# A hybrid decoder layer on one core: projection quarters handed out in pieces during the sparse attention

## The reference

```
o_cmp: softmax over 63 compressed keys (computed ahead, outside the loop changed here)
o_slc: softmax over the selected blocks of 64 keys among all keys up to the row's own
o_win: softmax over a window of 512 keys
o = gt[0] * o_cmp + gt[1] * o_slc + gt[2] * o_win
```

## Time and profile before

| | us |
|---|---|
| median of three runs (lowest, highest) | 2026.82 (2026.44, 2088.94) |
| the profiled execution's own time | 2009.73 |
| its span, first to last instruction | 2007.6 |
| PE busy in the span | 1955.3 (97%) |
| DVE busy in the span | 1342.2 (67%) |
| ACT busy in the span | 928.1 (46%) |
| POOL busy in the span | 612.7 (31%) |

### The profile page before, as it was taken

One profiled execution on the slowest core, in us unless ns is written; L12 is line 12 of the kernel. 1 busy time (PEld: TensorE's weight loads), 2 busy tenths in 40 slices (PEclk: granted clock), 3 DMA queues, 4 the chain that ended last, 5 costly groups with the idle time before them and its releaser, 6 DMA issues. The chain is left out here.

```text
span 2007.6 us, 32329 instructions
## 1 busy us (share of the span) xinstructions
PE 1955.3 (97%) x9421; PEld 1474.9 (73%) x9422; DVE 1342.2 (67%) x2558; ACT 928.1 (46%) x1615; POOL 612.7 (31%) x403
## 2 busy tenths in 40 slices
PE   8999999999999999999999989999999999999996
PEld 7887787877768766658868647777777777677772
DVE  2794643444206677789867838788778787777776
ACT  2111221234212244451034347777777777677764
POOL 2443232223322221002142733333333333233321
PEclk9999999999999999999999999999999999999998
DMA  6122312132532211047770577999999999999986
GB/s 205 42 70 88 105 43 63 43 87 56 123 101 80 85 53 33 22 135 260 241 292 34 204 275 233 312 377 343 327 344 325 352 326 343 317 319 333 342 270 178
DMA packets 170899, 390.66 MB, mean 195 GB/s; under 512 B 27937, under 2 KB 100930, under 8 KB 146113
## 3 DMA queue, kind: packets, MB, share of 16 engines
q1 hardware_dynamic: 132032, 302.71, 41.6%
q0 software_dynamic: 29568, 70.09, 14.0%
q10 hardware_dynamic: 9216, 16.78, 2.2%
HBM read 338.58 MB, written 81.84 MB: 209 GB/s over the span
## 5 line engine op out<-in xcount | busy, mean ns | idle before, releaser
L649 PE MATMUL a_bank<-x_hi,w_hi 128*128 128x512 f32 x928 | 372.9, 402 | 0.0
L649 PE MATMUL a_bank<-x_hi,w_lo 128*128 128x512 f32 x928 | 362.4, 390 | 0.0
L649 PE MATMUL a_bank<-x_lo,w_hi 128*128 128x512 f32 x928 | 361.5, 390 | 0.0
L2368 DVE TENSOR_TENSOR u_lo<-w_gu,u_hi 128x1024 fp32r<-128x1024 f32 x225 | 268.1, 1219 | 37.6 <-ACT u_hi L2010 29.6
L2010 ACT ACTIVATE u_hi<-w_gu 128x1024 fp32r x225 | 230.6, 1065 | 19.2 <-SPq L1497 18.7
L584 POOL CAST w_hi<-w_raw 128x1024 fp32r<-128x1024 f32 x56 | 64.8, 1158 | 560.2 <-PE a_bank L649 539.5
L2383 DVE TENSOR_TENSOR d_lo<-w_d,d_hi 128x1024 fp32r<-128x1024 f32 x150 | 177.1, 1222 | 83.0 <-ACT d_hi L2118 81.0
L1800 PE MATMUL e_bank<-u_hi,x_g_hi 128*128 128x512 f32 x450 | 207.5, 461 | 0.0
L649 PEld LDWEIGHTS a_bank<-x_hi,w_hi 128*128 128x128 f32 x928 | 174.3, 188 | 40.7 <-issue 6.1
L649 PEld LDWEIGHTS a_bank<-x_hi,w_lo 128*128 128x128 f32 x928 | 174.2, 188 | 37.8
L649 PEld LDWEIGHTS a_bank<-x_lo,w_hi 128*128 128x128 f32 x928 | 174.6, 188 | 33.9 <-issue 0.5
(11 more groups left out here) (397 smaller groups left out, 3657.3 us busy)
## 6 DMA issues: line engine op xcount, KB each, us to landing
w_gu<-in_moe_wg SPq DMA_DIRECT2D x64, 1024.0 KB, 8.5
w_gu<-in_moe_wu SPq DMA_DIRECT2D x64, 1024.0 KB, 27.2
w_d<-in_moe_wd SPq DMA_DIRECT2D x64, 1024.0 KB, 25.5
w_raw<-in_w_in SPq DMA_DIRECT2D x53, 512.0 KB, 3.9
gates<-gate_out ACTq DMA_DIRECT2D x64, 256.0 KB, 2.0
g_sb<-gates SPq DMA_DIRECT2D x16, 1024.0 KB, 5.5
acc_odd<-zero POOLq DMA_DIRECT2D x9, 512.0 KB, 14.9
work<-in_w_out SPq DMA_DIRECT2D x4, 1024.0 KB, 8.1
```

The lines of the kernel that those rows point to most:

```text
L649: ins = pe.matmul(bank[h][:, :], w[:, c % 2, k, :], x[:, k, cols], start=(k == 0 and j == 0), stop=(k == KD - 1 and j == 2))
L2368: dve.tensor_tensor(up_part(u_lo[j]), up_weights(slot, j), up_part(u_hi[j]).bitcast(F32), ALU.subtract).then_inc(u_lo_dve, 1)
```

## The change

In the NSA loop the quarters go out in pieces of one contraction slice (three matmuls) each. The schedule gets items `('mm_k', q, k)` for the four pieces of quarter q, and the item `('mm', q)` behind the fourth, at which PE no longer computes anything but ACT and POOL do what they did. The number of pieces behind the groups of pair k-1 is 120 (four times the quarters left) times the pair's weight over 99. The weight of a pair is one plus its number of groups, and 99 is the sum over the first 30 pairs. The sliding-window loop keeps whole quarters at rate 2. Rounds -1 and 0 of NSA keep `adv(1)`.

```diff
-    state = dict(q=4, fill=0, pv=0)
+    state = dict(q=4, k=0, fill=0, pv=0)
...
+
+    def adv_k(n):
+        for _ in range(n):
+            if state['q'] < last:
+                items.append(('mm_k', state['q'], state['k']))
+                state['k'] += 1
+                if state['k'] == 4:
+                    items.append(('mm', state['q']))
+                    state['q'], state['k'] = state['q'] + 1, 0
...
-    def attention(pairs, rate):
+    def attention(pairs, rate, step):
...
-                    debt += rate / len(groups)
-                    adv(int(debt))
+                    debt += rate(pairs, k) / len(groups)
+                    step(int(debt))
                     debt -= int(debt)
...
-    attention(SWA, 2.0)
+    attention(SWA, lambda pairs, k: 2.0, adv)
...
-    attention(NSA, (last - state['q']) / (len(NSA) - 2))
-    adv(last)
+    pieces = 4 * (last - state['q'])
+    weight = [1 + (pr['nb'] + 1) // 2 for pr in NSA]
+    attention(NSA, lambda pairs, k: pieces * weight[k - 1] / sum(weight[:-2]), adv_k)
+    adv_k(4 * last)
     return items
 
 
 SCHEDULE = schedule()
+PIECES_FROM = next(item[1] for item in SCHEDULE if item[0] == 'mm_k')
...
-            def quarter(q):
+            def quarter(q, ks=range(4)):
 
                 c, h, part = q // 4, q // 2 % 2, q % 2
-                if q == 0:
-                    pe.wait_ge(w_first_hi, 1)
-                    pe.wait_ge(w_first_lo, 1)
-                elif q == 1 or q % 4 == 0:
-                    pe.wait_ge(w_hi_ready, c + 1)
-                    pe.wait_ge(w_lo_ready, c + 1)
-                if q < 4:
-                    pe.wait_ge(x_lo_ready, 4 * q + 4)
-                if part == 0 and c >= 1:
-                    pe.wait_ge(half_out, 2 * c + h - 1)
-                for k in range(4 * part, 4 * part + 4):
+                if 0 in ks:
+                    if q == 0:
+                        pe.wait_ge(w_first_hi, 1)
+                        pe.wait_ge(w_first_lo, 1)
+                    elif q == 1 or q % 4 == 0:
+                        pe.wait_ge(w_hi_ready, c + 1)
+                        pe.wait_ge(w_lo_ready, c + 1)
+                    if q < 4:
+                        pe.wait_ge(x_lo_ready, 4 * q + 4)
+                    if part == 0 and c >= 1:
+                        pe.wait_ge(half_out, 2 * c + h - 1)
+                for k in (4 * part + i for i in ks):
...
-                if part == 1:
+                if part == 1 and 3 in ks:
                     ins.then_inc(half_done, 1)
...
                 if what == 'mm':
-                    quarter(item[1])
+                    if item[1] < PIECES_FROM:
+                        quarter(item[1])
+                elif what == 'mm_k':
+                    quarter(item[1], item[2:])
```

## The result

The changed kernel takes 2027.81 us (median of 20 runs, 2023.80 to 2093.24) against 2025.07 us of the kernel before on the same chip (median of 20, 2019.23 to 2090.49). The ratio is 1.0019 with a 95% interval of 1.0012 to 1.0026: 3.8 us slower, where 5 us faster were forecast. In part of the executions of either kernel the clock is lower in the first 500 us and the time some 63 us longer; ratios leave these out, and the loop, which lies behind that stretch, can be read in them too.

A forecast was written before the change was run, and what follows sets the result against it. PE, busy 97% of the span, and its waits were taken as the bound. Gains of 10.0 us less 2.2, 1.6 and 0.8 made 5.4, called 5: from the median 2026.82 to 2021.8 us, range 2004 to 2031.

The forecast's parts named there:

- Prices on PE: PE times read from the trace: matmul spacing 0.232 us, a lone piece 0.87 including 0.17 for breaking off and resuming.
- step 1: Rounds 1 to 28: 34 groups without a quarter get pieces that fill PE's wait for ACT's copy; 7.9 us gained.
- Step 2: Three pieces leave rounds 1 to 28 for round 29: 2.1 us less on PE up to pair 30's scores.
- Step 3: Early rounds stripped of pieces become shorter on PE than on DVE in rounds 1, 4, 7, 8, 12: 2.2 us lost.
- Step 4: Round 29 with three pieces takes 6.8 us, DVE starts pair 31 later, and the loop's end is 1.6 us later.
- Step 5: POOL's splits hold DVE multiplies in rounds 1 to 8: 0.8 us more than before, 2.8 at most.
- PE's clock stayed at 1.00 ... so early waits of 0.5 us should not move it: PE's clock held at the 2.4 GHz level even where busy 7.74 of 10 us; no cost put on it.
- DVE held by POOL: Line 1217 in rounds without slack: seven splits may each hold a multiply 1.4 us; 4 us slower, 2031; chance 0.08.
- The gain is eaten: A cut costs 0.15 us more, 5.1 in all, or branch loads come 4 us late: 2026 to 2027; chance 0.22.
- a piece over 1.0 us: Sign of a wrong forecast: a lone piece takes over 1.0 us from its first matmul to the product.
- waits past round 16: Sign of a wrong forecast: a round past 16 shows PE waiting for DVE's line 1217.
- late loads: Sign of a wrong forecast: the first branch projections behind the loop wait for loads; up to 4 us given back.

The follow-up runs named there:

- the even kernel: Changed kernel with four pieces in every round instead of shares by weight: 2017.19 us, ratio 0.9965 to the kernel before.
- the kernel without holds: Changed kernel with POOL's subtraction cut to one of eight slices for every split in the loop, plus 12 dummy transposes ahead of pair 30: 2013.45 us (one run).
- the dummies: 12 transposes that nobody reads, added ahead of pair 30's first group; on the changed kernel 2024.07 us, ratio 1.000 to the kernel before.
- The shorter subtraction: Changed kernel, POOL's subtraction on one of eight slices for every split in the loop, with dummy transposes ahead of pair 30: 2013.45 us (one run).
- the short subtraction: Changed kernel with POOL's subtraction cut to one of eight slices, the loop's first split spared, no added dummy transposes: 2024.69 us (one run).
- last pieces in round 30: Changed kernel with even pieces up to round 28, none in round 29, the last three in round 30, no added dummies: 2020.57 us, ratio 0.999.

## Why the prediction was wrong

**Prices on PE and step 1 (7.9 us for 34 groups): right.** A lone piece took 0.86 us, and the even kernel gained 7.8 us up to pair 30's scores, 0.7 of it by a piece that left.

**Step 2 (2.1 us): right.** Steps 1 and 2 gave 176.3 us up to pair 30, PE's rounds sum to 176.0, and the kernel without holds had 179.0 with DVE's share in it.

**Step 3 (2.2 us where DVE is longer): right in size, partly in another place.** Without holds rounds 2, 4, 5, 7 and 8 took 0.9, 0.1, 0.7, 0.2 and 0.6 us more than PE's prices, 2.5 in all; rounds 1 and 12, where I had put 0.9 of it, lost nothing. What DVE lacks in one round reaches PE in the next.

**Step 4 (round 29 at 6.8, end 1.6 us later): right for round 29, wrong behind it.** 6.81 us. With the dummies round 29 and the end take 27.21 us together, where the forecast had 27.3; without them the pause of PE grew from 1.85 to 2.19 us, and the clock fell behind it.

**Step 5 (0.8 us more for POOL's splits, 2.8 at most): this is the step that failed.** The shorter subtraction gave back 6.4 us up to pair 30, 4.8 by held multiplies in three rounds (1.34, 1.66 and 1.8) and 1.6 by the clock behind the third. Two faults are in it. I looked for splits in rounds 1 to 8 only. The third held multiply, the norm of pair 12, is work of DVE in round 12, and my own step 3 has that round as one in which DVE is longer (5.4 against 5.0); PE stands for it at the start of round 13. Without the hold that norm's second multiply ends at 744.01 us and PE's transposes start at 744.15, so there was no slack for a hold of 1.8 us. And I took the value at the low end, from a row in which part of the hold was covered by slack (0.83 of 1.4), although the change takes just that slack away. The rule that I quoted beside it, the Trainium skill, "SBUF — State Buffer", section "Who interferes with whom", pointed to the upper end. The trace agrees with it: every multiply that started during a subtraction in the early rounds ended within 0.3 us of the subtraction's end, and the norm multiply of pair 12 beside a subtraction of 0.46 us took 0.55 us, as it does alone.

**"PE's clock stayed at 1.00 ... so early waits of 0.5 us should not move it": wrong.** The early waits were 1.8 to 2.3 us, since step 5 was wrong, and one of them brought the clock down, 1.6 us in round 13. The pause at the loop's end has nothing to do with step 5 (it is 2.19 us with the short subtraction too), and the forecast put no term on it: 4.1 us. The one profile I had showed a pause of 1.85 us without a fall; a second execution of the same kernel showed the same pause with one. I took a stretch of one execution for a property of the kernel.

**Sum.** Forecast 5.4 less; the loop of the changed profile is 4.9 more than in the first profile, 1.8 more than in the second of the same kernel, and the ratio says 3.8. The difference of 10.3 to the first profile is 6.1 up to pair 30 (step 5, with the clock in round 13) and 4.15 behind pair 31 (the clock).

**Rivals.** The slower one, "DVE held by POOL", had the right mechanism, place and sign, with a chance of 0.08. Its point of decision was four holds reaching PE; three were enough, because the clock added as much again. (Six splits start in the loop, not the seven that I counted.) That the time came out slower than before is thus by two costs, of which this rival named one. "The gain is eaten" came near in the time (2026 to 2027) but for causes that didn't occur: cuts cost what the row said, and the loads were not late. What I had named as showing the forecast wrong (a piece over 1.0 us, waits past round 16, late loads) did not show either. The range held the time of 2027.81 us, by the spread of the level and not by the sum: that is luck.

## What to carry to other kernels

A filler that is moved out of short rounds takes the other engine's slack with it. Before it is moved, count every long operation that can stop that engine (here one weight split per four quarters), put its full length against the slack left in each round and not only in those where the engine is already the bound, and give the filler out so that the slack stays. Here four pieces in every round gave the gain (0.35%, and 0.41% with the dummies), and following the number of groups took it away. Price a pause of PE with the clock that may fall behind it, and take a second profile before calling a stretch free of it.

## What was not expected of the hardware

- The same pause may or may not bring the clock down. Pauses of 2.16 and 2.17 us (round 2): no fall in the changed kernel's profile, 0.66, 0.66 and 0.52 in the following 4 us in three others with the same work there. 2.26 us (round 8): no fall in three profiles. 1.80 us (round 13): 0.58 to 0.65 in the same three. So the shorter pause brought the clock down each time and the longer one never. 1.85 us at the loop's end of the kernel before: 1.00 in one execution, 0.66 over 10 us in another. 1.94 us (last pieces in round 30): 0.57 over 888 to 892 us. What decides between them is open.
- A fall costs more than the pause: at the loop's end 4.2 us in the changed kernel (24.64 against 20.41), 3.2 in the same stretch with the short subtraction (23.56), 3.1 in the kernel before. Twelve dummy transposes, in time that PE would have spent waiting, took it away at the loop's end in all five kernels that had them.
- POOL's cast, 1.0 us ahead of each subtraction, goes with stretched multiplies too: 0.95 us for 640 keys where the neighbour took 0.61, and 1.30 for 768. With the subtraction shortened these two stayed as they were (0.95 and 1.30 us), and each ended 0.3 to 0.5 us behind the cast, much as a multiply held by a subtraction does. So the cast holds too, for its shorter length.
